# A hybrid encoder layer: low parts of six weight units and four gate products made by GpSimd

## The chip, the cores and the metric

The kernel runs on one core of a Trainium2 chip. The metric is the device time of one execution in microseconds (us); the time of a kernel is the median of several executions. TensorE is called PE here, VectorE DVE, ScalarE ACT, GpSimd POOL and SyncE SP, as in the profile.

## What is computed

The reference is one inference step of a two-layer encoder for 256 prompt frames and 64 sample frames, 320 tokens in all, with a model width of 1024. All data is float32.

```python
def _layer(x, l, P, ...):
    h = _rms_norm(x, P['ffn1_norm_pre'][l])
    x = x + 0.5 * _rms_norm(_swiglu(h, w_up, w_down), P['ffn1_norm_post'][l])
    h = _rms_norm(x, P['mix_norm_pre'][l])
    m, ... = _mixer(h, l, P, ...)
    x = x + _rms_norm(m, P['mix_norm_post'][l])
    h = _rms_norm(x, P['ffn2_norm_pre'][l])
    x = x + 0.5 * _rms_norm(_swiglu(h, w_up, w_down), P['ffn2_norm_post'][l])

def _mixer(h, l, P, ...):
    z = h @ P['w_in'][l]                        # 1024 -> 3344, split in 12 pieces
    ...
    o_a = _rms_norm(o_a, P['gla_norm'][l]) * jax.nn.silu(gr)      # GLA, 256 columns
    o_d = _rms_norm(o_d, P['diff_subln'][l]) * (1.0 - lam_init)   # attention, 512 columns
    o_r = _layer_norm(o_r, P['ret_norm'][l]) * jax.nn.silu(rg)    # retention, 256 columns
    out = jnp.concatenate([o_a, o_d, o_r], axis=-1) @ P['w_out'][l]
```

The change concerns the last three lines: the products with `silu(gr)` and `silu(rg)`, and the product with `w_out`.

## The kernel before

Activations lie transposed: 128 features on the partitions and 320 tokens along the free axis, so that `x` and `y` are 8 tiles of 128 x 320. Every matrix product is made from split operands. A value is divided in a high part (rounded to the type fp32r) and a low part (the rest), and `product` (L579) issues three matmuls of 128 x 128 weights on 320 columns: high weights by low data (L582), low weights by high data (L583), high by high (L584).

Weights come in units of 128 output columns by 1024 rows. A unit goes through one of six slots. SP loads it into `raw`. ACT's `hi` (L922, the instruction is L929) rounds it into `w_h` and counts up the semaphore `w_hi`. DVE's `lo` (L931, the instruction is L938) subtracts `raw - w_h` and writes `w_l`, which lies on top of `raw`; it counts up `w_lo`. PE waits on `w_lo`, multiplies, and frees the slot by `w_used`. All three counters count units in one order, so a unit's `lo` has to come behind that of the unit before it.

The mixer of a layer has 27 units of the input projection (`U_MIX + v`) and then 8 of the output projection (`U_OUT + v`). PE, ACT, DVE and POOL all walk the same hand-written list, `SCHEDULE` (L74), and each does what it has to do for an entry. An entry `("part", v, k0, k1)` is a stretch of unit v's matmuls. Where it ends the unit, DVE reads the result out of PSUM (`z_tile`, L1524, as L1532 or L1534), then makes the low part of the unit four further on. So parts 23 to 26 are followed by the `lo` of output units 0 to 3. Entry `("ahead",)` makes those of units 4 and 5.

Between the parts lies the rest of the mixer. For attention block n, `att_s` has PE make scores (L834 or L840), DVE add a bias and take the maximum (L1429, L1432), and ACT take the exponential (L1108). `att_a` is DVE's scaling: L1441, then L1445 and L1447 for prompt blocks, or L1449 for sample blocks. `att_t` is PE's transposes (L847), which wait for `att_a`. `att_o` is PE's product with the values (L860). `tok` are transposes (L748) and their copy by ACT; after `tok 7` POOL issues four stores of the new keys and values (L550, L553).

The end of the mixer normalises the eight tiles of `y`, one after the other in the order `HEAD_ORDER` = 2, 3, 4, 0, 1, 6, 7, 5. ACT squares the tiles; `stat` has PE sum them (L870, 42 small matmuls), ACT take a root and DVE the reciprocal. `spread n` has PE spread the factors of tile n over the partitions (L881), and DVE multiply the tile by its gain and these factors (L1500). Tiles 0, 1, 6 and 7 (GLA and retention) are then also multiplied by their gate (L1505), after ACT's entry `gates`, one Silu over four tiles (L1139). ACT rounds the tile into `xw_h`, and `lo n` makes its low part `xw_l` (L1241). `out i` has PE multiply the i-th tile of the order with output units 0 to 3. Units 4 to 7 follow as whole tiles. `spread` of the j-th tile waits for the scaling of tile j - 2 of the order, since two PSUM banks alternate.

POOL has little to do in the mixer: the decays and weighted keys of GLA (L493, L502) early in the list, some stores, and outside the list `x + y` (L473) and sums of squares (L481).

Of the kernel before, what the change touches and what calls it, by code (L numbers as in the profile page):

```python
# [50 lines left out]

HEAD_AT = ((0, 2, "head64"), (2, 2, "head64"), (8, 1, "head128"), (9, 1, "head128"), (10, 1, "head128"), (11, 1, "head128"),
           (4, 2, "head64"), (6, 2, "head64"))
HEAD_ORDER = (2, 3, 4, 0, 1, 6, 7, 5)
STAT_HEADS = {"a": (0, 1, 6, 7, 2, 3, 4), "b": (5,)}
STAT_COLS = {"a": (0, 11), "b": (11, 12)}
# [45 lines left out]
def milestones():  # L102
    pe, act, dve, pool = [], [], [], []
    for kind, *arg in SCHEDULE:
        n = arg[0] if arg else None
        if kind == "past":
            pe.append(f"kct{n}")
            act.append(f"kct{n}")
        elif kind in ("tok", "ret_kt"):
            pe.append(f"{kind}{n}")  # L110
            act.append(f"{kind}{n}")
        elif kind == "logit":
            pe.append("logit")
            act += ["abs", "softplus"]
            dve += ["minus", "decay"]
            pool += ["dist0", "dist1"]
        elif kind == "weight":
            act.append(f"weight{n}")
            pool.append(f"qk{n}")
            if n < 6:  # L120
                pool.append(f"dist{n + 2}")
        elif kind == "level":
            pe.append(f"level{n}")
            dve.append(f"score{n}")
        elif kind == "gla_keys":
            act += ["from_start", "to_end"]
            dve += ["q_start", "k_end"]
        elif kind == "ketok":
            pe.append("ketok")
            act.append("ketok")  # L130
        elif kind in ("gla_state", "ret_state"):
            pe.append(kind)
            dve.append(kind)
        elif kind in ("gla_o", "rot", "ret_s", "ret_o"):
            pe.append(f"{kind}{n}")
            dve.append(f"{kind}{n}")
        elif kind == "ret_mu":
            pe.append(f"ret_mu{n}")
            dve.append(f"ret_xc{n}")
        elif kind == "ret_dec":  # L140
            dve.append("ret_dec")
        elif kind == "att_s":
            pe.append(f"att_s{n}")
            dve.append(f"att_max{n}")
            act.append(f"att_e{n}")
        elif kind == "att_a":
            dve.append(f"att_a{n}")
        elif kind == "att_t":
            pe.append(f"att_t{n}")
            act.append(f"att_t{n}")  # L150
        elif kind == "att_o":
            pe.append(f"att_o{n}")
            if n % 3 == 2:
                act.append(f"att_o{n}")
        elif kind == "squares":
            act.append(f"squares_{n}")
        elif kind == "stat":
            pe.append(f"ms_{n}")
            act.append(f"sqrt_{n}")
            dve.append(f"inv_{n}")  # L160
        elif kind == "gates":
            act.append("gates")
        elif kind == "spread":
            pe.append(f"spread{n}")
            dve.append(f"head{n}")
    return {"pe": pe, "act": act, "dve": dve, "pool": pool}
# [69 lines left out]
def build(nc, ins, outs, table_at):  # L236
    ctx = ExitStack()
    with ctx:
# [110 lines left out]
        def slot(l, u):  # L349
            return (l * UNITS + u) % SLOTS  # L350
# [113 lines left out]
            return 16 * ((l * UNITS + u) // SLOTS + 1)  # L464


        @block.gpsimd
        def _(pool):
            def add_y(l, m):
# [35 lines left out]
            for l in range(DEPTH):  # L505
# [20 lines left out]
                for kind, *arg in SCHEDULE:  # L526
                    n = arg[0] if arg else None
                    if kind == "logit":
                        dist(l, 0)
                        dist(l, 1)  # L530
                    elif kind == "past" and n == 1:
                        after(pool, l, "pe", "kct1")
                        then_pass(pool)
                        pool.memset(scores[:, :, :, :], 0.0).then_inc(mem_set, 1)
                    elif kind == "weight":
                        qk(l, n)
                        if n < 6:
                            dist(l, n + 2)
                    elif kind == "gla_state":
                        after(pool, l, "dve", "gla_state")  # L540
                        then_pass(pool)
                        for i, name in enumerate(("prompt", "sample")):
                            pool.dma_start(outs[f"state_gla_{name}"][bass.ds(l, 1), 0].rearrange("a h d v -> (a h d) v"),
                                           st_a[:, i, :]).then_inc(st_stored, 16)
                    elif kind == "tok" and n == 7:
                        after(pool, l, "act", "tok7")
                        then_pass(pool)
                        for t, name in ((dk_tok, "k"), (dv_tok, "v")):
                            o = outs[f"new_{name}_prompt"]
                            pool.dma_start(o[bass.ds(l, 1), 0].rearrange("a (i p) h d -> p (a i) (h d)", p=P),  # L550
                                           t[:, 0:2, :, :].rearrange("p i h d -> p i (h d)")).then_inc(kv_stored, 16)
                            o = outs[f"new_{name}_sample"]
                            pool.dma_start(o[bass.ds(l, 1), 0].rearrange("a p h d -> p (a h d)"),  # L553
                                           t[64:128, 2, :, :].rearrange("p h d -> p (h d)")).then_inc(kv_stored, 16)
                    elif kind == "ret_state":
                        after(pool, l, "dve", "ret_state")
                        then_pass(pool)
                        for i, name in enumerate(("prompt", "sample")):
                            pool.dma_start(outs[f"state_ret_{name}"][bass.ds(l, 1), 0].rearrange("a (j h) d v -> (a h d) j v", j=2),
                                           st_r[:, i, :, :]).then_inc(st_stored, 16)  # L560
# [15 lines left out]
        def _(pe):  # L576
# [313 lines left out]
            for l in range(DEPTH):  # L890
# [17 lines left out]
                stat_y(l, 3, 1)  # L908
                spread(l, 3)
                ffn(l, U_F2, G_F2, 4, 3, 2)  # L910

        def blocks_of(u):

            if U_F1 + N_UP <= u < U_MIX or U_F2 + N_UP <= u < UNITS:
                a, z_ = THIRD[(u - (U_F1 if u < U_MIX else U_F2) - N_UP) % 3]
                return z_ - a
            return KD  # L920

        def hi(act, l, u, i=0):  # L922

            if u >= UNITS:
                l, u = l + 1, u - UNITS
            if l < DEPTH:
                s, cols = slot(l, u), blocks_of(u) * P
                act.wait_ge(raw_in[s], 16 * i + landed(l, u))
                act.activation(w_h[s][:, 0:cols], raw[s][:, 0:cols], ACT.Copy).then_inc(w_hi, 1)  # L929

        def lo(dve, l, u, i=0):  # L931

            if u >= UNITS:
                l, u = l + 1, u - UNITS
            if l < DEPTH:
                s, cols = slot(l, u), blocks_of(u) * P
                dve.wait_ge(w_hi, 6 * i + (l * UNITS + u + 1))
                dve.tensor_tensor(w_l[s][:, 0:cols], raw[s][:, 0:cols], w_h[s][:, 0:cols], ALU.subtract).then_inc(w_lo, 1)  # L938

# [248 lines left out]
        def _(dve):  # L1190
# [179 lines left out]
            def mixer_step(l, kind, n):  # L1370
# [123 lines left out]
                elif kind == "spread":  # L1494
# [2 lines left out]
                    after(dve, l, "pe", f"spread{n}")  # L1497
                    if n == 5:
                        after(dve, l, "act", "att_o11")
                    i = dve.scalar_tensor_tensor(y[:, n, :], y[:, n, :], smalls[l][:, gains_at[n]:gains_at[n] + 1],  # L1500
                                                 ps[:, 4 + HEAD_ORDER.index(n) % 2, 0:T], ALU.mult, ALU.mult)
                    if n in (0, 1, 6, 7):
                        dve.drain()
                        after(dve, l, "act", "gates")
                        i = dve.tensor_tensor(y[:, n, :], y[:, n, :], z[:, GR + n if n < 2 else RG + n - 6, :], ALU.mult)  # L1505
                    mark("dve", i, f"head{n}")
                elif kind == "lo":
                    split_lo(l, 2, n, y, None, HEAD_ORDER.index(n))
                elif kind == "ahead":
                    for v in (4, 5):  # L1510
                        lo(dve, l, U_OUT + v)

            for l in range(DEPTH):
                begin(l, 0, 0, 0, U_F1, l > 0)
# [25 lines left out]
                for kind, *arg in SCHEDULE:  # L1540
                    if kind == "part":
                        v, k0, k1 = arg
                        if k1 == KD:
                            z_tile(v)
                            lo(dve, l, U_MIX + v + 4)
                    else:
                        mixer_step(l, kind, arg[0] if arg else None)
                dve.memset(ssum[:, :], D * EPS / P)
                for v in range(N_OUT):
                    if v < KD - 1:  # L1550
                        add_square(l, v, 1, v % 2)
                    if v < 5:
                        lo(dve, l, U_OUT + 6 + v)
                    if v == N_OUT - 2:
# [42 lines left out]
```

## Time and profile before

| | |
|---|---|
| median of 3 runs | 1440.01 us (1437.98 to 1443.89) |
| profiled execution, own time | 1441.2 us |
| span of its profile | 1439.4 us |
| mean granted TensorE clock | 0.977 |
| PE busy | 1369.2 us, 95% |
| DVE busy | 812.5 us, 56% |
| ACT busy | 625.0 us, 43% |
| POOL busy | 122.7 us, 9% |

The profile is of one execution. "Busy" is time in which an engine carries out an instruction, waiting for a blocked path included. Matmuls overlap one another, so their listed durations are longer than the distance between them. The mixer's end in layer 0 lies between 395 and 482 us, that of layer 1 between 1101 and 1188 us.

### The profile page before, as it was taken

To read this page: it belongs to the slowest core of one execution; us is meant where nothing else is said; L and a number is where in the kernel's file an instruction comes from. 1 tells how busy PE (TensorE), PEld (TensorE's weight loads), DVE (VectorE), ACT (ScalarE), POOL (GpSimd) and SP (SyncE) were. 2 spreads that over 40 slices of the span, in tenths; PEclk is the share of its full clock that TensorE was granted. 3 is DMA by queue.
4 is the path that set the end of the run, shared out by engine and by line. 5 is a ranking of instruction groups with operands and counts; after the bars stand their busy time and mean duration, and the time that the engine had idled before them with its cause. 6 is when DMAs were issued, how large, how long until landed. Compare 5 with 4: busy or idle time off the path is not lost.

```text
span 1439.4 us, 24605 instructions
## 1 busy us (share of the span) xinstructions
PE 1369.2 (95%) x9589; PEld 1331.6 (93%) x9589; DVE 812.5 (56%) x1226; ACT 625.0 (43%) x987; POOL 122.7 (9%) x119
## 2 busy tenths in 40 slices
PE   5999999899999899999989999998899999999998
PEld 5999999887799899999989999988788999999998
DVE  5565544568654765554366555346765557655542
ACT  4444433552353654443354444346234455444343
POOL 0000000341000200000020000013500002000000
PEclk9999999999999999999999999999999999999999
DMA  5955445433241365545545555454232343555452
GB/s 145 272 147 153 143 146 150 123 99 88 80 125 46 97 182 151 153 140 148 153 115 147 147 146 149 149 172 104 61 89 78 110 118 102 146 149 154 140 147 75
DMA packets 351289, 188.50 MB, mean 131 GB/s; under 512 B 6188, under 2 KB 348472, under 8 KB 350968
## 3 DMA queue, kind: packets, MB, share of 16 engines
q1 hardware_dynamic: 348368, 177.49, 43.9%
q0 software_dynamic: 1872, 6.88, 1.4%
q10 hardware_dynamic: 984, 3.22, 0.7%
q8 instruction: 45, 0.74, 0.2%
q14 instruction: 20, 0.16, 0.0%
HBM read 183.25 MB, written 4.33 MB: 130 GB/s over the span
## 4 chain that ended last, share of the span: by engine, by line
PE 86%; DVE 6%; DMA 3%; ACT 2%; DVEq 1%; issue 1%; POOL 0%; ACTq 0%; SPq 0%; POOLq 0%
PE ps L582 26%; PE ps L584 26%; PE ps L583 25%; DMA raw<-in_ffn_w_up_dram 2%; DVE scores L1399 2%; DVE w_l L938 1%; DMA raw<-in_w_in_dram 1%; PE ps L860 1%; PE ps L870 1%; PE ps L638 1%; PE ps L763 1%; PE ps L834 0%; PE ps L748 0%; DVE y L1254 0%; PE ps L881 0%
## 5 line engine op out<-in xcount | busy, mean ns | idle before, releaser
L582 PE MATMUL ps<-xn_l,w_h 128*128 128x320 f32 x1840 | 588.2, 320 | 25.4 <-DVE xn_l L1243 18.2
L583 PE MATMUL ps<-xn_h,w_l 128*128 128x320 f32 x1840 | 576.4, 313 | 0.0
L584 PE MATMUL ps<-xn_h,w_h 128*128 128x320 f32 x1840 | 576.3, 313 | 0.0
L938 DVE TENSOR_TENSOR w_l<-raw,w_h 128x1024 fp32r<-128x1024 f32 (+1 forms) x342 | 412.5, 1208 | 185.0 <-ACT w_h L929 184.9
L929 ACT ACTIVATE w_h<-raw 128x1024 fp32r<-128x1024 f32 (+1 forms) x342 | 353.4, 1035 | 278.3 <-DMA raw<-in_ffn_w_down_dram 125.2
L582 PEld LDWEIGHTS ps<-xn_l,w_h 128*128 128x128 f32 x1840 | 353.2, 192 | 35.7 <-DVE xn_l L1243 19.6
L583 PEld LDWEIGHTS ps<-xn_h,w_l 128*128 128x128 f32 x1840 | 353.5, 192 | 0.8 <-issue 0.2
L584 PEld LDWEIGHTS ps<-xn_h,w_h 128*128 128x128 f32 x1840 | 353.1, 192 | 0.0
L582 PE MATMUL ps<-hid_l,w_h 128*128 128x320 f32 x704 | 217.4, 309 | 0.0
L584 PE MATMUL ps<-hid_h,w_h 128*128 128x320 f32 x704 | 217.3, 309 | 0.0
L583 PE MATMUL ps<-hid_h,w_l 128*128 128x320 f32 x704 | 217.3, 309 | 0.0
L582 PEld LDWEIGHTS ps<-hid_l,w_h 128*128 128x128 f32 x704 | 132.2, 188 | 0.0
L583 PEld LDWEIGHTS ps<-hid_h,w_l 128*128 128x128 f32 x704 | 132.2, 188 | 0.0
L584 PEld LDWEIGHTS ps<-hid_h,w_h 128*128 128x128 f32 x704 | 132.2, 188 | 0.0
L1306 DVE TENSOR_TENSOR gate<-ps,rs 128x320 f32<-128x320 f32 x72 | 35.3, 490 | 147.4 <-PE ps L584 147.1
L1012 ACT ACTIVATE gate<-gate 128x320 f32<-128x320 f32 x72 | 33.9, 471 | 136.1 <-DVE gate L1306 136.0
L473 POOL TENSOR_TENSOR x<-x,y 128x320 f32<-128x320 f32 x35 | 36.8, 1084 | 357.8 <-DVE y L1254 357.8
L1016 ACT ACTIVATE hid_h<-up 128x320 f32 (+1 forms) x72 | 34.0, 472 | 67.4 <-DVE up L1312 67.4
L1532 DVE TENSOR_TENSOR z<-ps,rs 128x320 f32<-128x320 f32 x38 | 18.3, 485 | 45.5 <-PE ps L584 45.5
L997 ACT ACTIVATE sq<-ps 128x320 f32<-128x320 f32 x48 | 20.9, 436 | 53.0 <-PE ps L584 53.0
L582 PE MATMUL ps<-xw_l,w_h 128*128 128x320 f32 x128 | 40.4, 315 | 2.5 <-DVE xw_l L1241 2.5
L1108 ACT ACTIVATE probs<-probs,tiny 128x128 f32<-128x128 f32 (+2 forms) x40 | 19.2, 481 | 53.8 <-DVE tiny L1432 53.8
(223 smaller groups left out, 1165.8 us busy)
## 6 DMA issues: line engine op xcount, KB each, us to landing
raw<-in_ffn_w_up_dram SPq DMA_DIRECT2D x176, 512.0 KB, 3.9
raw<-in_ffn_w_down_dram SPq DMA_DIRECT2D x64, 448.0 KB, 3.7
raw<-in_w_in_dram SPq DMA_DIRECT2D x54, 512.0 KB, 3.8
raw<-in_ffn_w_down_dram SPq DMA_DIRECT2D x32, 512.0 KB, 3.9
raw<-in_w_out_dram SPq DMA_DIRECT2D x16, 512.0 KB, 4.1
const<-in_tables_dram ACTq DMA_DIRECT2D x1, 2176.0 KB, 10.7
mask_in<-in_masks_dram POOLq DMA_DIRECT2D x1, 1536.0 KB, 11.7
x_in<-in_x_prompt_dram SPq DMA_DIRECT2D x1, 1024.0 KB, 3.6
```

Source lines behind the costliest of these rows:

```text
L473: pool.tensor_tensor(x[:, k, :], x[:, k, :], y[:, k, :], ALU.add).then_inc(x_new, 1)
L582: pe.matmul(out, w_h[s][:, w], xl, start=first, stop=False)
L583: pe.matmul(out, w_l[s][:, w], xh, start=False, stop=False)
L584: return pe.matmul(out, w_h[s][:, w], xh, start=False, stop=last)
L929: act.activation(w_h[s][:, 0:cols], raw[s][:, 0:cols], ACT.Copy).then_inc(w_hi, 1)
L938: dve.tensor_tensor(w_l[s][:, 0:cols], raw[s][:, 0:cols], w_h[s][:, 0:cols], ALU.subtract).then_inc(w_lo, 1)
L997: act.activation(sq[b][:, :], ps[:, bank, 0:T], ACT.Square).then_inc(y_sq, 1)
L1012: act.activation(gate[q][:, :], gate[q][:, :], ACT.Silu).then_inc(silu, 1)
L1016: act.activation(tile(hid_h, v), up[q][:, :], ACT.Copy).then_inc(hid_hi, 1)
L1108: i = act.activation(p, p, ACT.Exp, bias=tiny[:, 8 + 2 * s + m:9 + 2 * s + m], accum_out=tiny[:, 12 + 2 * s + m:13 + 2 * s + m])
L1306: dve.tensor_tensor(gate[q][:, :], ps[:, 2 * q, 0:T], rs[:, :], ALU.mult).then_inc(up_mul, 1)
L1399: i = dve.copy_predicated(flat[:, :, a:b], m, ps_m[:, :, a:b])
```

## The change

The functions `hi` and `lo` move up in the file, so that POOL can call `lo` too; their text stays. POOL makes the low parts of output units 0 to 5: unit 0 at the end of part 23, units 1 and 2 at the end of parts 24 and 25, units 3 and 4 at the end of part 26, unit 5 at `ahead`. It waits first until DVE has made that of the last input unit, and DVE waits for POOL's six before it goes on with output unit 6. At entry `gates` POOL multiplies tiles 0, 1, 6 and 7 of `y` by their gates. DVE's scaling of such a tile (`spread`) waits for that and no longer multiplies by the gate itself.

```diff
+GATED = (0, 1, 6, 7)
...
         elif kind == "gates":
             act.append("gates")
+            pool += [f"gated{q}" for q in GATED]
...
@@ POOL @@
+                    elif kind == "part" and n + 4 >= N_MIX and arg[2] == KD:
+                        if n + 4 == N_MIX:
+                            pool.wait_ge(w_lo, l * UNITS + U_OUT)
+                        lo(pool, l, U_MIX + n + 4)
+                        if n == N_MIX - 1:
+                            lo(pool, l, U_OUT + 4)
+                    elif kind == "gates":
+                        after(pool, l, "act", "gates")
+                        for q in GATED:
+                            mark("pool", pool.tensor_tensor(y[:, q, :], y[:, q, :], z[:, GR + q if q < 2 else RG + q - 6, :], ALU.mult),
+                                 f"gated{q}")
+                    elif kind == "ahead":
+                        lo(pool, l, U_OUT + 5)
...
@@ DVE @@
+                    if n in GATED:
+                        after(dve, l, "pool", f"gated{n}")
                     i = dve.scalar_tensor_tensor(y[:, n, :], y[:, n, :], smalls[l][:, gains_at[n]:gains_at[n] + 1],
                                                  ps[:, 4 + HEAD_ORDER.index(n) % 2, 0:T], ALU.mult, ALU.mult)
-                    if n in (0, 1, 6, 7):
-                        dve.drain()
-                        after(dve, l, "act", "gates")
-                        i = dve.tensor_tensor(y[:, n, :], y[:, n, :], z[:, GR + n if n < 2 else RG + n - 6, :], ALU.mult)
                     mark("dve", i, f"head{n}")
...
-                elif kind == "ahead":
-                    for v in (4, 5):
-                        lo(dve, l, U_OUT + v)
...
                         if k1 == KD:
                             z_tile(v)
-                            lo(dve, l, U_MIX + v + 4)
+                            if v + 4 < N_MIX:
+                                lo(dve, l, U_MIX + v + 4)
...
                 for v in range(N_OUT):
                     if v < KD - 1:
                         add_square(l, v, 1, v % 2)
+                    if v == 0:
+                        dve.wait_ge(w_lo, l * UNITS + U_OUT + 6)
                     if v < 5:
                         lo(dve, l, U_OUT + 6 + v)
```

## Rows read from the trace of the kernel before

**Rows 1.** The page: busy us, share of the span and instructions of each engine.
```profile
PE 1369.2 (95%) x9589; PEld 1331.6 (93%) x9589; DVE 812.5 (56%) x1226; ACT 625.0 (43%) x987; POOL 122.7 (9%) x119
```

**Rows 2.** PE's waits in the run: us in total, times, longest.
```profile
PE ps L582 <- DVE w_l L938: 3.0, 2, 2.4
...
PE ps L847 <- DVE probs L1449: 0.3, 1, 0.3
```

**Rows 3.** Timeline of PE, layer 0: start, us, instruction.
```profile
414.17 0.38 PE L847 MATMUL ps<-const,probs 128*128 128x128 f32 x2
...
419.72 0.70 PE L834 MATMUL ps<-z 64*128 64x256 f32 x4
...
425.31 0.27 PE L847 MATMUL ps<-const,probs 128*128 128x128 f32 x1
```

**Rows 4.** POOL's L473 and L568: count, duration in ns min/median/max, first and last start.
```profile
L473 POOL TENSOR_TENSOR x<-x,y x35: 847/1122/1132, 264.8 to 1195.3; 128x320 f32<-128x320 f32 x35
...
L568 POOL TENSOR_TENSOR const<-const,x_in x2: 1264/1265/1266, 1433.5 to 1434.8; 128x512 f32<-128x512 f32 x2
```

**Rows 5.** Timeline of DVE in the mixer's end, layer 0.
```profile
409.61 1.21 DVE L938 TENSOR_TENSOR w_l<-raw,w_h 128x1024 fp32r<-128x1024 f32 x1
...
412.06 0.41 DVE L1445 TENSOR_SCALAR probs<-probs,tiny,par 128x256 f32<-128x256 f32 x1
...
421.04 0.68 DVE L1429 SCALAR_TENSOR_TENSOR probs<-const,ps 128x512 f32<-128x512 f32 x1
...
422.63 0.35 DVE L1445 TENSOR_SCALAR probs<-probs,tiny,par 128x128 f32<-128x128 f32 x1
423.06 0.35 DVE L1447 SCALAR_TENSOR_TENSOR probs<-probs,tiny 128x128 f32<-128x128 f32 x1
...
440.00 0.48 DVE L1449 TENSOR_SCALAR probs<-probs,tiny,par 128x384 f32<-128x384 f32 x1
...
449.74 0.55 DVE L1500 SCALAR_TENSOR_TENSOR y<-y,par,ps 128x320 f32<-128x320 f32 x1
451.81 0.49 DVE L1505 TENSOR_TENSOR y<-y,z 128x320 f32<-128x320 f32 x1 [1.52 <-ACT z L1139]
```

**Rows 6.** Timeline of POOL in the GLA part, layer 0.
```profile
316.52 1.55 POOL L502 TENSOR_TENSOR sq<-z,ssum 128x640 f32<-128x640 f32 x1 [1.47 <-ACT ssum L1085]
318.15 1.58 POOL L493 TENSOR_TENSOR ssum<-decay 128x320 f32<-128x320 f32 x1
...
324.71 0.72 POOL L493 TENSOR_TENSOR ssum<-decay 128x320 f32<-128x320 f32 x1
```

**Rows 7.** Timeline of DVE beside it.
```profile
316.86 2.29 DVE L938 TENSOR_TENSOR w_l<-raw,w_h 128x1024 fp32r<-128x1024 f32 x1
```

**Rows 8.** DVE by shape: instructions, busy us, mean ns of one.
```profile
L1447 DVE SCALAR_TENSOR_TENSOR probs<-probs,tiny 128x256 f32<-128x256 f32 x8 | 3.9, 484 | 0.7
...
L1445 DVE TENSOR_SCALAR probs<-probs,tiny,par 128x256 f32<-128x256 f32 x8 | 3.3, 412 | 0.6
```

**Rows 9.** Timeline of POOL: the last of its four stores of keys and values, layer 0.
```profile
420.81 0.56 POOL L553 DMA_DIRECT2D out_new_v_sample_dram<-dv_tok  x1
```

**Rows 10.** Timeline of ACT, layer 0.
```profile
435.07 1.04 ACT L929 ACTIVATE w_h<-raw 128x1024 fp32r<-128x1024 f32 x1
...
450.50 1.27 ACT L1139 ACTIVATE z<-z 128x1280 f32<-128x1280 f32 x1
```

**Rows 11.** Timeline of PE at the gates, layer 0.
```profile
452.44 0.88 PE L881 MATMUL ps<-const,inv_h 128*64 128x128 f32 x12
453.47 0.88 PE L881 MATMUL ps<-const,inv_h 128*64 128x128 f32 x12
454.27 0.41 PE L582 MATMUL ps<-xw_l,w_h 128*128 128x320 f32 x1
```

**Rows 12.** PE in windows of 2 us: length, busy (count), granted clock, DMA share, GB/s.
```profile
432.00:434.00 2.00, 2.00 (x11) 0.50 0.00 0
...
442.00:444.00 2.00, 0.77 (x5) 1.00 0.00 0
```

More of the change, by code:

```diff
@@ L464, in landed, with blocks_of, hi, lo @@
             return 16 * ((l * UNITS + u) // SLOTS + 1)
+        def blocks_of(u):
+            if U_F1 + N_UP <= u < U_MIX or U_F2 + N_UP <= u < UNITS:
+                a, z_ = THIRD[(u - (U_F1 if u < U_MIX else U_F2) - N_UP) % 3]
+                return z_ - a
+            return KD
+        def hi(act, l, u, i=0):
+            if u >= UNITS:
+                l, u = l + 1, u - UNITS
+            if l < DEPTH:
+                s, cols = slot(l, u), blocks_of(u) * P
+                act.wait_ge(raw_in[s], 16 * i + landed(l, u))
+                act.activation(w_h[s][:, 0:cols], raw[s][:, 0:cols], ACT.Copy).then_inc(w_hi, 1)
+        def lo(dve, l, u, i=0):
+            if u >= UNITS:
+                l, u = l + 1, u - UNITS
+            if l < DEPTH:
+                s, cols = slot(l, u), blocks_of(u) * P
+                dve.wait_ge(w_hi, 6 * i + (l * UNITS + u + 1))
+                dve.tensor_tensor(w_l[s][:, 0:cols], raw[s][:, 0:cols], w_h[s][:, 0:cols], ALU.subtract).then_inc(w_lo, 1)
         @block.gpsimd
@@ L910, in _ @@
                 ffn(l, U_F2, G_F2, 4, 3, 2)
[L915 to L938, printed above, removed]
         @block.scalar
```

## The prediction

> **What bounds the kernel now.** I read the page's table of engines first. TensorE (PE) is busy for 95% of the span, VectorE (DVE) for 56%, GpSimd (POOL) for 9% [rows 1]. Work taken off DVE is therefore worth only what PE waits for it. So I looked next at the list of PE's waits. PE waits for a low part (`w_l`, L938) twice in the run, 3.0 us in all, and once for DVE's attention scaling (L1449), 0.3 us [rows 2]. None of PE's long waits is one that DVE's `lo` of an output unit ends. Last I read PE's own timeline in the stretch where the change works: its attention transposes (L847) follow the weight tiles at once, with no idle time in front of them [rows 3]. The mixer runs once per layer, and both layers show the same pattern, so every price below counts twice. A DVE made shorter here can give back only the 0.3 us, in one layer. The change can, on the other hand, add waits, and that is where the numbers lie.
>
> **Price of one POOL instruction.** No subtraction of 1,024 columns stands on POOL in this trace. The nearest rows have two SBUF inputs and other widths. 320 columns took 0.847 us at the least (the median of 1.12 us holds waiting), and 512 columns took 1.265 us [rows 4]. The slope is 0.418 us over 192 columns, 2.18 ns a column. So 1,024 columns should take 1.265 + 512 x 0.00218 = 2.38 us, where DVE needs 1.21 us [rows 5]. A gate product of 320 columns takes 0.85 us. The low bound for the subtraction is 2.3 us (a little less slope). The high bound is the slowest row stretched, 1.12 x 1024 / 320 = 3.6 us; it would hold if writing the rounded type costs POOL more. I take 2.38, since the two clean rows give it.
>
> **POOL and DVE block each other.** At 316.52 POOL starts a product. At 316.86 DVE starts a `lo`, with two SBUF inputs, and takes 2.29 us where it takes 1.21 alone: it waits to 318.07, when POOL ends, and then runs [rows 6, 7]. POOL's next instruction starts at 318.15 and takes 1.58 us where its like takes 0.72: now POOL waits for DVE [rows 6]. So one of the two holds the path for its whole instruction, and the one that waits gets it next. Which DVE instructions in the attention part would wait? L1447 has two SBUF inputs, so it would. L1445, a scaling with one SBUF tensor, takes 0.35 us for 128 columns and 0.412 us for 256. That is about 0.5 ns a column, while L1447 takes 0.35 and 0.484 us [rows 5, 8], about 1.0 ns a column. L1445 moves two elements where L1447 moves one, so it draws on as much SBUF width as an instruction with two inputs; I take it as blocked too. No row shows an L1445 beside a running POOL, so both cases are kept.
>
> The Trainium skill ("SBUF — State Buffer", section "Who interferes with whom") says the same of both kinds: a VectorE instruction in a two-port mode, or with two SBUF inputs against a GpSimd instruction that reads SBUF, fully blocks or is blocked. By it the sum is that with L1445 blocked; without it, that with L1447 alone.
>
> **Units 0 to 4.** *Unit 0* (part 23). POOL waits until DVE's own last `lo` ends, 409.61 + 1.21 = 410.82 [rows 5], and then runs to 413.2. DVE asks for L1445 at 412.06 and is held to 413.2. From the start of L1445 to the end of L1447 it needed 0.98 us (412.06 to 413.04), so it ends at 414.2. PE takes its transpose at 414.17 [rows 3, 5]. Cost: 0.05 us.
>
> *Units 1 and 2* (parts 24 and 25). POOL's four stores of keys and values come before unit 1 in its order, and the last issue ends at 420.81 + 0.56 = 421.37 [rows 9]. `w_h` of both units is there in time. So POOL subtracts unit 1 from 421.4 to 423.8 and unit 2 straight behind it. DVE, without its own `lo`, reaches L1429 as soon as PE's scores are there, at 419.72 + 0.70 = 420.42 [rows 3], say 420.5 in place of 421.04. L1445 stood 1.59 us behind L1429 and so asks at 422.1. It is held to 423.8 and ends at 424.15. POOL's unit 2, which waited for it, runs from about 424.1 to 426.5. L1447 asks at 424.2, is held to 426.5 and ends at 426.85. PE's transpose L847, which stands at 425.31 [rows 3] with the weight tile before it just done, starts at 426.9. Queued behind L1447 on DVE is `z_tile`, and behind the transpose on PE everything else. Cost, unit 0's included: about 1.55 us a layer. If L1445 is not blocked, it ends at 422.5 and L1447 is held to 423.8 alone, ends at 424.15, and PE loses nothing here: 0.05 us in all. With a subtraction of 2.38 + d us the cost is 1.55 + 3d (unit 0 pushes PE by d, units 1 and 2 by d each).
>
> *Units 3 and 4* cost nothing. Between part 25 and part 26 PE has its 42 small statistics products, and DVE nothing urgent. Unit 4 follows `w_h`, which ACT ends at 435.07 + 1.04 = 436.11 [rows 10], and so ends near 438.6, or 440.0 with the shift. DVE's L1449 would ask 1.5 us later than its 440.00 less the 1.1 of the `lo` that is gone [rows 5], near 440.4. If that cover were gone the cost would be a few tenths. The missing `lo` ahead of L1449 removes PE's 0.3 us wait of [rows 2], once.
>
> **The gates.** ACT ends the Silu at 450.50 + 1.27 = 451.77 [rows 10]. Before, DVE has head 0 scaled by then (449.74) and only multiplies, from 451.81 [rows 5]; PE's L881 for head 6 starts at 452.44, for head 7 at 453.47, and output step 3 at 454.27 [rows 11]. After, POOL multiplies head 0 to about 452.7 and head 1 to 453.55. DVE scales behind each for 0.55 us: head 0 to 453.3, head 1 to 454.15. With the same 0.14 us to PE, L881 starts at 453.4 and 454.3, and step 3 0.80 us behind that, at 455.1. Cost: 0.85 us a layer. At 1.12 us for a product, the median of [rows 4], it is 1.3. Heads 6 and 7 come from POOL by 455.8 at the latest, even if `xw_l` of head 0 gets in between; they are needed a whole output step later. Behind them the order is as before, moved by 0.85 us.
>
> **Unit 5 and the end of the stage.** Unit 5 is multiplied only after the last four output steps and the whole tile of unit 4, so 1.2 us more for its subtraction (2.38 less 1.21) hides under that work of PE; without it those 1.2 us would show. DVE's new wait in front of unit 6 holds only adds of squares, and unit 6 itself waits for its load. No DMA is added or moved past another; the stores on POOL's queue wait for ACT longer than unit 0 lasts.
>
> **The sum.** 2 x 1.55 + 2 x 0.85 - 0.3 = 4.5 us. Against the profiled execution's own time of 1441.2 us that is 1445.7. The median of the three timed runs, 1440.0, lies 1.2 below that execution, so I forecast **1444.5 us**, 0.3% longer. About 0.5% (7.2 us) is what a measurement of this kernel can tell from no change, so this counts as the same.
>
> **Rivals.**
> 1. *L1445 is not blocked.* For it: it has one SBUF tensor, and no row shows it beside POOL. Against it: its rate. The sum is 0.1 + 1.7 - 0.3 = 1.5 us, 1441.5. Chance 0.25.
> 2. *Slower by over 0.5%: POOL needs more than the clean rows say for a rounded output.* Its place is units 0 to 2, where the sum is 4.5 + 6d. It passes 7.2 us from d = 0.45, a subtraction of 2.83 us. At the high bound of 3.6 us it gives 4.5 + 7.3 = 11.8 us, 1451.8. For it: no row has POOL write this type. Against it: DVE's `lo` of this type costs what its column count says. Chance 0.10.
> 3. *The longer idle time costs TensorE its clock.* The granted clock is 0.50 (1.2 GHz) in 432 to 434, behind 3 us of small products, and 1.00 (2.4 GHz) in 442 to 444, where PE is busy for only 0.77 of 2 us [rows 12]. After the change the idle time at 452 is some 1.3 us, no longer than that at 442, which the clock outlived; this speaks against. About 7 us at half clock in both layers would cost 2 x 3.5 us more: 1451.5. Chance 0.05.
> 4. *The relief of DVE gives back more than I see.* PE has one wait of 0.3 us to give, so a gain of 7.2 us would need a source that no view shows. Chance 0.03. My forecast itself: 0.57.
>
> **How the numbers follow.** The likeliest case gives 1444.5. Cases 1 and 2 bound the range: 1441.5 less 1.5 us of spread between medians (the three runs span 5.9 us) is 1440, and a subtraction of 2.8 us with the gates at their high price gives about 1448.5, with the spread 1449.5. Faster 0.03; slower is rivals 2 and 3, 0.15 less a part that stays under the line, 0.13; same 0.84.
>
> **What the new profile would show.** Right: POOL's L938-like subtraction at 2.4 us, twelve of them; L1447 near 2.6 us long once per layer; a PE wait of 1.5 us in front of L847 ended by DVE's `probs`; PE's wait ahead of L881 for DVE `y` of about 1 us. Wrong: a DVE scaling that keeps 0.35 us beside a running POOL (rival 1), subtractions of 3 us or more (rival 2), a granted clock under 1.00 around 452 to 460 (rival 3). The forecast also falls if POOL issues unit 1 later than 421.4, since then unit 2 might end behind PE's next need, or if POOL, not DVE, wins the path between two POOL instructions.

## The result, and the profile after

The changed kernel takes 1445.39 us (median of 20 runs, 1441.51 to 1450.81), the kernel before 1439.91 us (20 runs, 1437.98 to 1447.59). The ratio is 1.0032, with a 95% interval of 1.0022 to 1.0042: 4.6 us longer (3.2 to 6.0), within the 7.2 us that count as no change, and real all the same. The forecast was 0.3% longer.

The profiled execution is one of the quick ones: its span is 1439.9 us, 0.5 us over that of the kernel before. It is read here for what each wait costs in its place; what happens to the rest is taken up below. In the changed kernel the line numbers are others: L1457 is the old L1445 (scaling with one tensor), L1459 the old L1447 (two tensors), L887 the old L847 (PE's transposes), L921 the old L881 (the spreads), L1514 the old L1500 (DVE's product with gain and factors), L1253 the old L1241 (`xw_l`), L492 the subtraction of `lo`, L575 POOL's gate product.

PE's waits after, in the whole run (total us, times, longest):

```profile
PE ps L887 <- DVE probs L1459: 2.8, 2, 1.6
PE ps L622 <- DVE xw_l L1253: 2.5, 2, 1.2
PE ps L921 <- DVE y L1514: 2.4, 2, 1.2
```

The first and the last are new, one per layer each; the middle one, for `xw_l`, was 2.5 us before as well. The 0.3 us for L1449 of [rows 2] has gone. POOL's timeline in layer 0 shows what it does now:

```profile
411.05 2.39 POOL L492 TENSOR_TENSOR w_l<-raw,w_h 128x1024 fp32r<-128x1024 f32 x1 [34.18 <-DVE w_l L492]
...
421.88 4.72 POOL L492 TENSOR_TENSOR w_l<-raw,w_h 128x1024 fp32r<-128x1024 f32 x2
427.65 2.39 POOL L492 TENSOR_TENSOR w_l<-raw,w_h 128x1024 fp32r<-128x1024 f32 x1 [1.05 <-ACT w_h L483]
436.42 2.37 POOL L492 TENSOR_TENSOR w_l<-raw,w_h 128x1024 fp32r<-128x1024 f32 x1 [6.39 <-ACT w_h L483]
451.36 3.58 POOL L575 TENSOR_TENSOR y<-y,z 128x320 f32<-128x320 f32 x4 [12.56 <-ACT z L1151]
```

A subtraction takes 2.36 to 2.39 us, as the two clean rows of [rows 4] said (2.38); units 1 and 2 run without a gap, 4.72 us for two. And DVE beside it, to be compared with [rows 5]:

```profile
412.20 1.40 DVE L1457 TENSOR_SCALAR probs<-probs,tiny,par 128x256 f32<-128x256 f32 x1
...
420.62 0.69 DVE L1441 SCALAR_TENSOR_TENSOR probs<-const,ps 128x512 f32<-128x512 f32 x1 [0.48 <-PE ps L874]
...
422.22 4.47 DVE L1457 TENSOR_SCALAR probs<-probs,tiny,par 128x128 f32<-128x128 f32 x1
426.77 0.35 DVE L1459 SCALAR_TENSOR_TENSOR probs<-probs,tiny 128x128 f32<-128x128 f32 x1
```

The scaling with one SBUF tensor, 0.35 us before, lasts 4.47 us: it ends 0.1 us behind the end of POOL's second subtraction (421.88 + 4.72 = 426.60). Behind it L1459 runs at its own speed. What PE makes of this and of the gates:

```profile
414.30 0.38 PE L887 MATMUL ps<-const,probs 128*128 128x128 f32 x2
...
427.18 0.33 PE L887 MATMUL ps<-const,probs 128*128 128x128 f32 x1 [1.56 <-DVE probs L1459]
...
453.02 1.69 PE L921 MATMUL ps<-const,inv_h 128*64 128x128 f32 x24 [1.22 <-DVE y L1514]
```

The transpose of 425.31 in [rows 3] is at 427.18, and the one wait of 1.22 us in front of L921 stands where [rows 11] had a start at 452.44.

**Stage by stage.** The execution as a whole says little, since some stages differ from one execution to the next. So I measured three stretches in every profile, each from one instruction to another: A, from DVE's `z_tile` of part 22 to PE's 42 statistics matmuls; B, from there to `z_tile` of part 26; C, from there to DVE's reciprocal (L1250 before) that ends the mixer. For the kernel before in layer 0 these are 409.20 to 428.39, to 438.22, to 480.50.

| us, layer 0 / layer 1 | A | B | C |
|---|---|---|---|
| before | 19.19 / 19.19 | 9.83 / 9.50 | 42.28 / 42.28 |
| after | 20.99 / 20.63 | 8.18 / 9.07 | 42.36 / 43.12 |
| after, second execution | 21.01 / 20.63 | 8.20 / 9.04 | 42.36 / 43.12 |

A is 1.4 to 1.8 us longer, C up to 0.84 us. B is shorter, though nothing in it has changed but its time of arrival. Over both layers the three together are 2.1 us longer in the first execution (144.35 less 142.27) and in the second alike. (The second execution is that of the repeated run at the end of the experiments.)

### The profile page after: what moved, and what is told of

It is laid out like the page before. It is cut to its first block, busy times and chain, and to the rows that moved or that the text cites. A ratio compares the mean times of both kernels' runs of the same rounds, so it can differ in the third digit from the quotient of the medians.

```text
span 1439.9 us, 24609 instructions
## 1 busy us (share of the span) xinstructions
PE 1364.8 (95%) x9589; PEld 1328.5 (92%) x9589; DVE 807.1 (56%) x1206; ACT 625.3 (43%) x987; POOL 158.8 (11%) x139
## 3 DMA queue, kind: packets, MB, share of 16 engines
HBM read 183.25 MB, written 4.33 MB: 130 GB/s over the span
## 4 chain that ended last, share of the span: by engine, by line
PE 85%; DVE 7%; DMA 3%; ACT 2%; issue 1%; DVEq 1%; POOL 1%; ACTq 0%; SPq 0%; POOLq 0%
PE ps L622 26%; PE ps L624 25%; PE ps L623 25%; DMA raw<-in_ffn_w_up_dram 2%; DVE scores L1411 2%; DVE w_l L492 1%; DMA raw<-in_w_in_dram 1%; PE ps L900 1%; PE ps L910 1%; DVE probs L1457 1%; PE ps L921 1%; PE ps L803 1%; PE ps L678 1%; PE ps L874 0%; PE ps L788 0%
## 5 line engine op out<-in xcount | busy, mean ns | idle before, releaser
L492 DVE TENSOR_TENSOR w_l<-raw,w_h 128x1024 fp32r<-128x1024 f32 (+1 forms) x330 | 398.9, 1211 | 184.9 <-ACT w_h L483 184.8
L1120 ACT ACTIVATE probs<-probs,tiny 128x128 f32<-128x128 f32 (+2 forms) x40 | 19.2, 482 | 52.6 <-DVE tiny L1444 52.6
```

Of the source, the lines that this page charges most:

```text
L1120: i = act.activation(p, p, ACT.Exp, bias=tiny[:, 8 + 2 * s + m:9 + 2 * s + m], accum_out=tiny[:, 12 + 2 * s + m:13 + 2 * s + m])
```

## The experiments

### The two parts alone

The first kernel has the low parts on POOL and the gate products on DVE as before:

```diff
-            pool += [f"gated{q}" for q in GATED]
...
-                    if n in GATED:
-                        after(dve, l, "pool", f"gated{n}")
...
+                    if n in (0, 1, 6, 7):
+                        dve.drain()
+                        after(dve, l, "act", "gates")
+                        i = dve.tensor_tensor(y[:, n, :], y[:, n, :], z[:, GR + n if n < 2 else RG + n - 6, :], ALU.mult)
```

> POOL makes the low parts of output units 0 to 5, DVE multiplies by the gates as before the change. Theory (two separate costs: the blocked path in the attention part, 1.6 us a layer, and the later gates, 0.6 to 0.85 us a layer): PE's wait for DVE's L1459-type scaling stays at 1.2 to 1.6 us per layer, the wait in front of L921 falls back to 0.3 and 0.15 us; the time is 2.8 us over before (1.0019), less whatever the granted clock gives back behind the stall. Rival (the gates carry the cost): the time is within 1 us of before.

Measured: ratio 1.0018 (1.0003 to 1.0034), 2.6 us longer. A is 20.99 us in layer 0. The wait for the scaling is there as before, and the wait in front of L921 is not in the list at all:

```profile
PE ps L881 <- DVE probs L1453: 2.8, 2, 1.6
```

(L881 is this kernel's transposes, L1453 its scaling with two tensors.) In the profile, then, the cost stands without the gates on POOL. The interval alone (0.4 to 4.9 us) does not exclude the rival, that the gates carry the cost; the next kernel does.

The second kernel has only the gate products on POOL:

```diff
-                    elif kind == "part" and n + 4 >= N_MIX and arg[2] == KD:
...
-                    elif kind == "ahead":
-                        lo(pool, l, U_OUT + 5)
...
-                            if v + 4 < N_MIX:
-                                lo(dve, l, U_MIX + v + 4)
+                            lo(dve, l, U_MIX + v + 4)
...
+                elif kind == "ahead":
+                    for v in (4, 5):
+                        lo(dve, l, U_OUT + v)
```

> Only the four gate products are on POOL, all low parts are DVE's. Theory: no wait of PE for DVE's attention scalings beyond the 0.3 us of before; a wait of about 1.2 us per layer in front of L921 for DVE's y, and the time 1.2 to 1.7 us over before (1.0010). Rival (the gates carry the whole measured difference): 4.6 us over before (1.0032).

Measured: ratio 1.0001 (0.9983 to 1.0018), 0.1 us in a range of 2.5 to either side. In its profile A is 19.19 and 19.20 us, as before, and C is 43.18 and 43.17 us, 0.9 us a layer over before. PE's wait is that of the changed kernel:

```profile
PE ps L913 <- DVE y L1506: 2.4, 2, 1.2
```

So the profile shows 1.8 us for the gates, and the timing can neither confirm this nor tell it from nothing. The interval's upper end, 2.6 us, does exclude that they carry the whole 4.6 us.

### Unit 2 behind DVE's scaling

The changed kernel, with one wait for POOL ahead of unit 2:

```diff
+                        if n == 25:
+                            after(pool, l, "dve", "att_a9")
                         lo(pool, l, U_MIX + n + 4)
```

> The whole change, but POOL waits for DVE's attention scaling of block 9 before it subtracts unit 2. Theory (POOL holds the path over two subtractions in a row, 4.5 us, and that is what stalls PE): the tensor-scalar scaling is held by unit 1 alone, some 1.7 us, the scaling with two inputs takes 0.35 us, both end before PE's transposes need them, and PE's wait there is gone; the time is 1.0 to 1.7 us over before (1.0010). Rival (DVE is held by anything that POOL does in this stretch, also by its stores): the wait stays above 1 us and the time stays 4 to 5 us over before.

Measured: ratio 1.0004 (0.9989 to 1.0019), 0.6 us longer. The list of PE's waits has none for a scaling any more, and A is 19.22 us in both layers: the 1.4 to 1.8 us are gone. POOL and DVE in layer 0:

```profile
422.56 2.39 POOL L492 TENSOR_TENSOR w_l<-raw,w_h 128x1024 fp32r<-128x1024 f32 x1
425.55 2.38 POOL L492 TENSOR_TENSOR w_l<-raw,w_h 128x1024 fp32r<-128x1024 f32 x1 [0.61 <-DVE probs L1461]
```

```profile
422.87 2.16 DVE L1459 TENSOR_SCALAR probs<-probs,tiny,par 128x128 f32<-128x128 f32 x1
425.12 0.35 DVE L1461 SCALAR_TENSOR_TENSOR probs<-probs,tiny 128x128 f32<-128x128 f32 x1
```

Held by unit 1 alone, the scaling lasts 2.16 us (1.80 in layer 1), both are done at 425.47, and PE does not wait. POOL's stores are where they were, so the rival that they hold DVE is out too. What stalls PE is the second subtraction.

### A wait of POOL for itself

Why did L1457 not get in between units 1 and 2, as `lo` did in [rows 6, 7]? There POOL waits on a semaphore between two instructions. So this kernel has only such a wait, for POOL's own unit 1:

```diff
+                        if n == 25:
+                            pool.wait_ge(w_lo, l * UNITS + U_OUT + 2)
                         lo(pool, l, U_MIX + n + 4)
```

> The whole change, with one wait more: POOL waits for its own unit 1 to be finished before it starts unit 2. Theory (two POOL instructions that stand back to back keep the path over both; a wait between them gives it free, as in the GLA part): DVE's tensor-scalar scaling gets in behind unit 1 and lasts 1.6 to 2.2 us in place of 4.5, the scaling with two inputs is then held by unit 2 for about 2.3 us, and PE's wait for it stays near 1.6 us. Rival (POOL keeps the path whenever its next instruction is due): the tensor-scalar scaling stays at 4.5 us.

This kernel was run once, with a profile; its one time, 1445.72 us, decides nothing. DVE in layer 0:

```profile
423.44 2.15 DVE L1459 TENSOR_SCALAR probs<-probs,tiny,par 128x128 f32<-128x128 f32 x1
425.68 2.43 DVE L1461 SCALAR_TENSOR_TENSOR probs<-probs,tiny 128x128 f32<-128x128 f32 x1
```

The two durations are those that the prediction had worked out: 2.15 and 2.43 us, where the changed kernel has 4.47 and 0.35. The rival is out. Against this scaling, two POOL subtractions that follow each other with nothing to wait for hold the path as if they were one; a wait between them, even one that costs nothing, lets the scaling in. For PE it is nearly the same: its wait is 2.3 us in two layers instead of 2.8, and A is 20.76 and 20.41 us.

This does not hold for every DVE instruction. The changed kernel's four gate products follow each other without a wait too, and there DVE's subtraction for `xw_l`, with two SBUF inputs, got in between the third and the fourth (layer 0, three windows):

```profile
453.00 0.87 POOL L575 TENSOR_TENSOR y<-y,z 128x320 f32<-128x320 f32 x1
...
453.61 0.61 DVE L1253 TENSOR_TENSOR xw_l<-y,xw_h 128x320 fp32r<-128x320 f32 x1
...
453.82 1.11 POOL L575 TENSOR_TENSOR y<-y,z 128x320 f32<-128x320 f32 x1
```

It takes 0.46 us alone (at 448.82). Here it waits for the third product and is done at 454.22, while the fourth product runs to 454.94 and takes 0.25 us more than the others. Layer 1 and the four other profiles with gate products at this place show the same. So what DVE asks with matters as well as POOL's order. Whether it is the kind of instruction or the length of POOL's own is not tested.

### The gates earlier

The changed kernel, with the entry of the gates moved up by one output step, to a place where ACT idles:

```diff
-       ("lo", 4), ("gates",), ("spread", 0),
+       ("lo", 4), ("spread", 0),
...
-       ("lo", 2), ("out", 0),
+       ("lo", 2), ("out", 0), ("gates",),
```

> The whole change, with the entry of the gates moved up to just behind output step 0, so that ACT takes the Silu where it idles and POOL multiplies four heads while DVE idles. Theory: POOL's products end near 449.5 in layer 0, no engine waits for them, PE's 1.2 us in front of L921 disappears, also the 0.3 and 0.15 us that the kernel before had there; the stall in the attention part stays. The time is about 2.4 us over before (1.0017), 2.2 to 2.6 us under the changed kernel. Rival (ACT's reload of the root's table, 1.28 us, then lies on the path to the last statistics): a new wait for the spread of head 5, and no gain over the changed kernel.

Measured: ratio 0.9986 (0.9970 to 1.0002), 2.0 us under before in the middle of an interval that just includes no change, although the wait of 2.8 us for the scalings is still there. The expectation was 2.4 us over. C is 40.89 and 40.74 us: 1.4 to 1.5 us under before, where 0.45 had been counted as the waits to be removed. The rest is in ACT's timeline, shown for the next kernel.

### Both edits together

> The whole change with both edits: unit 2 behind DVE's scaling of block 9, and the gates just behind output step 0. Theory (costs add): neither PE wait is left, and neither are the waits of 0.3 us for the scaling of the last block and of 0.45 us for the gates that the kernel before has in a layer; the time is 1 to 2 us under before (0.999). If the earlier gates are worth more than the waits they remove, as the run with them alone suggests (2 us under before in spite of the stall of 2.8), it is 4 to 5 us under before (0.997).

Measured: 1436.26 us (12 runs), ratio 0.9971 (0.9960 to 0.9982). That is 4.2 us under the kernel before, and it beats the changed kernel by more: the intervals of 0.9971 and 1.0032 are far apart. A is 19.19 and 19.20 us, C 40.34 and 40.53. ACT's timeline of this kernel, layer 0 (two windows):

```profile
444.78 1.28 ACT L1153 ACT_TABLE_LOAD   x1
446.08 1.27 ACT L1153 ACTIVATE z<-z 128x1280 f32<-128x1280 f32 x1
...
449.27 1.28 ACT L1150 ACT_TABLE_LOAD   x1
450.64 0.27 ACT L1150 ACTIVATE var_h<-ps,const 128x3 f32<-128x3 f32 x1
```

```profile
480.84 0.17 ACT L988 ACTIVATE var<-ps 128x3 f32<-128x3 f32 x1 [0.74 <-PE ps L672]
```

and the end of the same stage before:

```profile
479.00 1.28 ACT L974 ACT_TABLE_LOAD   x1
480.30 0.17 ACT L974 ACTIVATE var<-ps 128x3 f32<-128x3 f32 x1
```

Before, the Silu is ACT's last function of another table, so the root that closes the mixer has to load its table first, on the path: the last statistics matmul ends at 479.73 and the root starts at 480.30. With the gates ahead of the last head's statistics, the root's table is loaded again at 449.27, beside PE's work, and stays. I read C's gain as three parts, from the start of `z_tile` of part 26: 0.77 us to output step 0 (DVE has no subtraction there; 5.01 before, 4.24 here), 0.58 us at the gates (from the spread of head 0 to that of head 5, 7.32 before, 456.14 less 448.82, and 6.73 here), and 0.53 us at the root (from the first of the last statistics matmuls to the reciprocal, 2.27 before, 1.74 here). They sum to 1.9 us of the 1.94 in layer 0. The three prices are read from one profile; no kernel separates the second from the third.

### Fewer units on POOL

This kernel has the early gates, and POOL makes only the low parts of output units 3 to 5, whose subtractions fall where PE needs no scaling soon:

```diff
-                    elif kind == "part" and n + 4 >= N_MIX and arg[2] == KD:
-                        if n + 4 == N_MIX:
-                            pool.wait_ge(w_lo, l * UNITS + U_OUT)
-                        lo(pool, l, U_MIX + n + 4)
-                        if n == N_MIX - 1:
-                            lo(pool, l, U_OUT + 4)
+                    elif kind == "part" and n == N_MIX - 1 and arg[2] == KD:
+                        pool.wait_ge(w_lo, l * UNITS + U_OUT + 3)
+                        lo(pool, l, U_OUT + 3)
+                        lo(pool, l, U_OUT + 4)
...
-                            if v + 4 < N_MIX:
+                            if v < N_MIX - 1:
                                 lo(dve, l, U_MIX + v + 4)
```

> DVE keeps the low parts of output units 0 to 2, POOL makes those of 3 to 5, and the gates stand just behind output step 0 on POOL. Theory: POOL does not touch the path while DVE scales blocks 7 and 9, so no scaling is longer than before, PE waits for none, and the time is that of the mended kernel within 1 us: 1 to 2 us under before (0.999). Rival (the relief of DVE by units 0 to 2 is worth something): 1 us or more over the mended kernel.

Measured: ratio 0.9984 (0.9973 to 0.9996), 2.3 us under before. The two intervals overlap, so the rival is neither shown nor excluded by the times. For the theory: A, where units 0 to 2 are made, is about 19.2 us in both kernels, so their place gives PE nothing there. Against its letter: one scaling is longer than before, that of block 10, held by unit 3 for 1.71 us in layer 0; PE does not wait for it.

### Is POOL needed for it?

Two kernels without one half each. The first is the kernel before with only the entry of the gates moved, as above; the second is the fewer units of the last experiment with gates late and on DVE.

> The kernel before, unchanged but for the place of the gates' entry (ACT's Silu just behind output step 0); DVE still makes all low parts and the gate products. Theory (the gain of the two earlier runs comes from ACT's order and not from POOL: the root's table is loaded behind the last square of the mixer and is still there for the stage's last root, 0.53 us, and the Silu is done before DVE needs it): PE's waits in front of L881 go, no table load stands ahead of the last root, and a layer is 0.9 to 1.1 us shorter; the time is about 2 us under before (0.9986). Rival (POOL's products are what makes the early gates pay): within 0.5 us of before.

Measured: ratio 0.9979 (0.9968 to 0.9991), 3.0 us under before. C is 40.89 and 40.88 us, 1.4 us a layer shorter. No table load stands ahead of the last root, and ACT waits there for PE:

```profile
482.36 0.17 ACT L974 ACTIVATE var<-ps 128x3 f32<-128x3 f32 x1 [0.50 <-PE ps L630]
```

The expected 0.9 to 1.1 us a layer was too little: from the start of PE's last weight matmul to the reciprocal it takes 1.91 us in both layers, against 2.72 before, so the root gives 0.81 us here and not 0.53; the other 0.6 us is at the gates. So ACT's order is worth 3.0 us with no work on POOL, the larger part of the 4.2 us of the kernel with both edits. The two intervals overlap, so the rest is not shown by the times.

> Only the low parts of output units 3 to 5 are POOL's; DVE makes those of units 0 to 2 and the gate products, and the gates stand where they stood. Theory (the wait of PE for DVE's scaling of the last block costs more than its 0.3 us in the list, since the matmuls behind it start into an empty array: 0.7 us in the mended kernel): the step from part 26 to output step 0 is 0.5 to 0.8 us shorter in each layer and the time is 1.0 to 1.5 us under before (0.9992). Rival (the listed 0.3 us in one layer is all): no change, within 0.3 us.

Measured: ratio 1.0004 (0.9992 to 1.0017): no gain that can be measured, the expected 1.0 to 1.5 us did not come. Its profile has 41.83 us for C in layer 0 and 42.50 in layer 1. From `z_tile` of part 26 to output step 0 it takes 4.21 us in layer 0, against 5.01 before, but 5.25 in layer 1, where the half clock of the statistics still holds in the spreads. Where PE is slow, DVE's subtraction was never what it waited for. The granted clock of this layer is 0.50 up to 1144, 1.4 us behind the start of `z_tile` of part 26 (1142.57); in layer 0 it is 0.99 from 438 to 440 (`z_tile` at 438.38). So relief of DVE is worth 0.8 us in a layer in which the clock has come back by then, and nothing in the other. Of the 0.8 us, 0.35 is lost again at the end of layer 0, where PE waits 0.5 us for DVE's sum of squares ahead of the last statistics.

### The changed kernel again

> The changed kernel once more, on the same chip as the others: 4 to 5 us over before (1.003), with the two PE waits of 1.2 to 1.6 us for the scalings and of 1.2 us in front of L921. If it comes out less than 2 us over before here, the larger part of the first difference was spread between the granted clocks of executions and not the change.

Measured: ratio 1.0025 (1.0010 to 1.0039), 3.6 us over before, the same two waits (2.8 us and 2.4 us in the run).

## Why the prediction was right

**The sum.** 4.5 us were forecast, 4.6 measured (3.2 to 6.0), and 3.6 when repeated. By terms, with what the profile shows:

| term | forecast, two layers | measured in the profile |
|---|---|---|
| scalings held by POOL (A) | +3.1 | +3.24 (1.80 + 1.44) |
| later gates | +1.7 | +1.8 (0.9 a layer, gates alone) |
| relief of DVE by unit 3 | -0.3 | -0.81 (0.78 + 0.03) |
| stretch B, the clock | 0 | -2.08 (1.65 + 0.43) |

**The price of POOL** held: 2.38 us forecast, 2.36 to 2.39 measured. Rival 2, a dearer rounded output, is out.

**Who blocks whom.** That the scaling with one SBUF tensor is held, worked out from its rate, is what the trace shows (1.40 us at unit 0, 4.47 at unit 1); rival 1 is out. The Trainium skill ("SBUF — State Buffer", section "Who interferes with whom") has the right pairs. It says that the path is kept "for the whole instruction"; against the scaling it was kept for two here (4.47 us), and the measurement decides.

**The wrong step inside a right sum** is "POOL's unit 2, which waited for it, runs from about 424.1 to 426.5". Unit 2 did not wait. I had drawn on [rows 6], where the one that waits gets in next, and did not see that POOL waits on a semaphore there. The prediction's last sentence names this case, POOL winning the path between two instructions, as one that would upset the forecast. It did not, because the two orders cost nearly the same. From the start of POOL's unit 1 to the end of the second scaling it takes 5.24 us in the changed kernel (421.88 to 427.12) and 5.00 us in the kernel with POOL's own wait, which has the forecast order (423.11 to 428.11); the forecast had 5.45 (421.4 to 426.85). That this term came out right is therefore partly luck.

**The gates** cost what was said: 0.85 us forecast, 0.9 measured in the kernel that has nothing else.

**The relief of DVE** was mis-sized: 0.3 us in one layer was forecast, 0.81 in both came, so rival 4 points the right way, by 0.5 us. The 0.3 us that the list gives PE's wait is not what its removal is worth: 0.78 us in layer 0. The list counts idle time only. In the kernel before, the transposes that follow the wait started 0.95 us behind PE's product with the values, in the mended kernel 0.44 us, and the next step came 0.22 us sooner too. In layer 1 the list has no wait there, and the step still went from 5.00 us to 4.33.

**What was not in the sum** is B. PE's clock is still granted in full (2.4 GHz) when the 42 small matmuls begin and falls to half (1.2 GHz) at some moment of this stretch that differs from execution to execution. Before, it is at half in 432 to 434 [rows 12]. After the change, in layer 0, it was still full at 432 to 434, some 2 us into the statistics, and fell in the next window, while it was at half there before:

```profile
432.00:434.00 2.00, 2.00 (x20) 1.00 0.00 0
434.00:436.00 2.00, 2.00 (x14) 0.74 0.00 0
```

Over all profiles B lies between 7.6 and 10.4 us. In the ten layers with a stall ahead of it (the changed kernel twice, the units alone, the early gates alone, POOL's own wait) its mean is 8.6 us, in the fourteen without one 9.5 us. This suggests that a stall is partly given back in B, but values of both groups overlap (8.1 to 10.4 without a stall), so I don't call it shown. The clock is not what makes the timed difference: its mean over the 12 repeated executions is 0.977, over the 29 of before beside them 0.976.

Nor is it settled how the timed 4.6 and 3.6 us go with the 2.1 us that the three stretches have in both profiled executions. That the first profile's span is only 0.5 us over that of before has its place: the stretch from the reciprocal of layer 0 to `z_tile` of part 22 in layer 1 takes 632.95 us after and 634.82 before. Part of this is PE's waits for GLA scores in layer 1 (1.4 us in one wait, 2.9 us in three before). Over the twelve profiles this stretch lies between 629.5 and 635.0 us, so one execution says little about the whole. Rival 3, a clock lost at the gates, is out: in layer 0 the clock is 1.00 in all windows of 2 us from 442 to 466.

**Arithmetic.** The upper end of the range was added up a little high: a subtraction of 2.8 us and the gates at their high price give 7.9 us, 1447.9 and not 1448.5. Nothing hangs on it.

## What to carry to other kernels

Work moved from DVE to POOL can take DVE's time as well: here it held DVE's instructions with two SBUF inputs and its scalings of one SBUF tensor at 0.5 ns a column. Look for what DVE has due in the next two to five microseconds, and let POOL wait for that before a second long instruction. Before moving arithmetic, look at ACT's order: the Silu one step earlier took a table load off the path and gave 3.0 us with no other engine touched, while moving three units alone gave nothing that could be measured. And a wait in the list may be worth more or less than its idle time, so it is worth one experiment that removes it alone.

## What the hardware showed that I had not expected

Two POOL subtractions without a wait between them kept a DVE scaling out for both: 4.47 us for one that takes 0.35, against 2.15 us when POOL waits for its own first result in between. A DVE subtraction with two SBUF inputs did get in between two POOL products without a wait (0.61 us in place of 0.46).

The same 42 matmuls of two columns took from 4.75 us (full clock to their end; early gates, layer 1) to 6.97 us (unit 2 late, layer 0). This alone moves a kernel by more than a microsecond per layer from one execution to the next, and it hides or feigns effects of that size in a single profile.
